# Differential attention: lambda's product moved to GpSimd, and VectorE's maxima and reciprocals put ahead of the difference and the lower halves

## The reference

```python
def diff_attention(q, k, v, lam):
    # q,k (B,H,2,S,d) holding (q1,q2)/(k1,k2); v (B,H,S,2d); causal
    ...
        logits = jnp.einsum('bhmqd,bhmkd->bhmqk', qi, k).astype(jnp.float32) * scale
        logits = jnp.where(kpos[None, :] <= qpos[:, None], logits, -jnp.inf)
        p = jax.nn.softmax(logits, axis=-1)
        pd = p[:, :, 0] - lam * p[:, :, 1]
        return jnp.einsum('bhqk,bhkd->bhqd', pd.astype(v.dtype), v)
```

## Time and profile before

| What | Value |
|---|---|
| median of 3 runs | 1244.85 us (1244.26 to 1247.47) |
| the profiled execution's own time | 1242.74 us |
| span of its trace | 1240.9 us |
| PE busy | 1202.0 us, 97% of the span |
| DVE busy | 748.2 us, 60% |
| ACT busy | 617.5 us, 50% |
| POOL busy | 139.8 us, 11% |
| differential stage | from about 218.3 us to 270.7 us of the span |

### The profile page before, as it was taken

One profiled execution on the slowest core, in us unless ns is written; L12 is line 12 of the kernel. 1 busy time (PEld: TensorE's weight loads), 2 busy tenths in 40 slices (PEclk: granted clock), 3 DMA queues, 4 the chain that ended last, 5 costly groups with the idle time before them and its releaser, 6 DMA issues.

```text
span 1240.9 us, 16231 instructions
## 1 busy us (share of the span) xinstructions
PE 1202.0 (97%) x6126; PEld 998.0 (80%) x6126; DVE 748.2 (60%) x1131; ACT 617.5 (50%) x1040; POOL 139.8 (11%) x217
## 2 busy tenths in 40 slices
PE   8999999989999999999999999999999999999997
PEld 6877788668888778888777888888898888888885
DVE  5556566764334364776276666445647848659478
ACT  5456686666233244643556544344347355354463
POOL 3023223110000011000033100010001000010011
PEclk9999999999999999999999999999999999999999
DMA  5422234113333535342113245312267474562732
GB/s 175 102 68 52 60 94 104 49 35 85 102 92 94 187 85 173 85 126 80 51 36 118 97 125 167 105 55 82 83 189 169 112 196 102 171 152 59 230 68 85
DMA packets 151740, 133.35 MB, mean 107 GB/s; under 512 B 5298, under 2 KB 124146, under 8 KB 151667
## 3 DMA queue, kind: packets, MB, share of 16 engines
q1 hardware_dynamic: 142528, 105.53, 28.9%
q0 software_dynamic: 3456, 12.58, 5.4%
q10 hardware_dynamic: 5682, 14.25, 3.3%
HBM read 115.55 MB, written 4.22 MB: 97 GB/s over the span
## 4 chain that ended last, share of the span: by engine, by line
PE 83%; DVE 8%; ACT 3%; DMA 3%; issue 1%; ACTq 0%; POOL 0%; POOLq 0%; DVEq 0%
PE lin L883 22%; PE lin L885 21%; PE lin L884 21%; DVE w_lo L2143 2%; PE tr L1041 2%; PE sc L885 2%; PE sc L884 2%; PE sc L883 2%; DVE neg_max L2168 1%; PE sc L1051 1%; PE tr L883 1%; PE tr L885 1%; PE tr L884 1%; PE sc L1053 1%; DMA x_m<-in_x 1%
## 5 line engine op out<-in xcount | busy, mean ns | idle before, releaser
L883 PE MATMUL lin<-h_hi,w_hi 128*128 128x512 f32 (+1 forms) x848 | 325.3, 384 | 5.0 <-DVE h_lo L2138 4.6
L885 PE MATMUL lin<-h_hi,w_lo 128*128 128x512 f32 (+1 forms) x848 | 317.4, 374 | 0.0
L884 PE MATMUL lin<-h_lo,w_hi 128*128 128x512 f32 (+1 forms) x848 | 317.0, 374 | 0.0
L2143 DVE TENSOR_TENSOR w_lo<-w_raw,w_hi 128x1024 fp32r<-128x1024 f32 x162 | 198.4, 1230 | 166.5 <-ACT w_hi L1452 154.9
L1452 ACT ACTIVATE w_hi<-w_raw 128x1024 fp32r<-128x1024 f32 x162 | 170.5, 1056 | 157.5 <-PE lin L885 53.7
L883 PEld LDWEIGHTS lin<-h_hi,w_hi 128*128 128x128 f32 x848 | 160.0, 189 | 33.7 <-DVE h_lo L2138 5.3
L885 PEld LDWEIGHTS lin<-h_hi,w_lo 128*128 128x128 f32 x848 | 159.8, 188 | 28.9
L884 PEld LDWEIGHTS lin<-h_lo,w_hi 128*128 128x128 f32 x848 | 160.2, 189 | 25.2 <-issue 0.2
L2168 DVE TENSOR_REDUCE neg_max<-sc 128x1 f32<-128x128 f32 (+3 forms) x112 | 52.2, 478 | 65.7 <-PE sc L1053 49.5
L1494 ACT ACTIVATE p<-sc,neg_max 128x128 f32<-128x128 f32 (+1 forms) x80 | 42.2, 528 | 72.6 <-DVE neg_max L2168 71.4
L883 PE MATMUL lin<-w_hi,h_hi 128*128 128x512 f32 x192 | 76.5, 398 | 1.2 <-DVE h_lo L2143 0.9
(11 more groups left out here) (354 smaller groups left out, 2310.0 us busy)
## 6 DMA issues: line engine op xcount, KB each, us to landing
w_raw<-in_w_in SPq DMA_DIRECT2D x74, 512.0 KB, 3.9
w_raw<-in_w_up SPq DMA_DIRECT2D x32, 512.0 KB, 4.4
wd_b<-in_w_down SPq DMA_DIRECT2D x24, 512.0 KB, 5.4
w_raw<-in_w_out SPq DMA_DIRECT2D x16, 512.0 KB, 3.5
w_raw<-in_w_xkv SPq DMA_DIRECT2D x16, 512.0 KB, 4.1
w_raw<-in_w_branch SPq DMA_DIRECT2D x8, 512.0 KB, 3.9
w_raw<-in_w_xq SPq DMA_DIRECT2D x8, 512.0 KB, 4.0
w_raw<-in_w_xo SPq DMA_DIRECT2D x8, 512.0 KB, 3.4
```

What stands on the lines that cost most here:

```text
L883: pe.matmul(o, lh, rh, start=start, stop=False)
L884: pe.matmul(o, lh, rl, start=False, stop=False)
L885: return pe.matmul(o, ll, rh, start=False, stop=stop)
L2143: return dve.tensor_tensor(out, x, as_f32(hi), ALU.subtract)
```

## The change

Five things are done. (1) On DVE the order inside a loop of the differential stage becomes maxima of w, reciprocals of w-1, difference of w-2, low part of w-5; before, the low part and the difference stood ahead of the maxima. (2) Lambda times the second reciprocal goes from DVE to POOL, 16 times, under a semaphore `lam_times`. (3) The first scores wait for their own head's queries and keys only, and the wait for the last tile of `vb` moves to the first value product; DVE takes that tile after the first maxima, and the weight split that followed it (of `zb`) moves some rounds into the stage on ACT and DVE; the same is done with the split after the second keys `ka` of fox. (4) ACT runs a one-column exponential after the forget gate and after the SiLU, and the table of exponentials is loaded there. (5) A group of `zb` filling is spread over 7 rounds and not 6.

```diff
-           "diff": [("zb", 0, 0, 6, 3)],
+           "diff": [("zb", 0, 0, 7, 3)],
...
             for w in range(16):
-                i, n = w % 4, P * (w % 4 + 1)
-                normalise(V0["diff"] + w, S0["diff"] + 2 * w, B["p0"][:, P_OFF[i]:P_OFF[i] + n])
+                i, n, s = w % 4, P * (w % 4 + 1), S0["diff"] + 2 * w
+                pool.wait_ge(s_rec, V0["diff"] + w + 1)
+                pool.tensor_scalar(rden[:, s + 1:s + 2], rden[:, s + 1:s + 2], neg_lam[:, :], 1.0, ALU.mult, ALU.mult)\
+                    .then_inc(lam_times, 1)
+                normalise(V0["diff"] + w, s, B["p0"][:, P_OFF[i]:P_OFF[i] + n])
...
-            pe.wait_ge(rope_lo, 8)
-            pe.wait_ge(k_twice, 16)
-            pe.wait_ge(dve_evac, DN[G["vb"][3]])
-
             def diff_scores(w):
                 h, i = w // 4, w % 4
+                if i == 0:
+                    pe.wait_ge(rope_lo, 5 + h)
+                    pe.wait_ge(k_twice, 8 + 2 * h + 2)
...
+                if h == 0:
+                    pe.wait_ge(dve_evac, DN[G["vb"][3]])
                 pe.wait_ge(tr_lo, R0["diff"] + 4 * h + 4)
...
+            def exponentials_next():
+
+                link(act.activation(act_one[:, :], ones[:, 0:1], ACT.Exp))
+
+            exponentials_next()
...
-            for c in range(2):
-                keys_hi("ka", c)
-                next_hi("ka", c)
+            keys_hi("ka", 0)
+            next_hi("ka", 0)
+            keys_hi("ka", 1)
...
+            def fox_exps(m):
+                causal_exps("fox", R0["fox"])(m)
+                if m == 4:
+                    next_hi("ka", 1)
...
             act.activation(B["y_1"][:, :, :], B["y_1"][:, :, :], ACT.Silu).then_inc(za_silu, 1)
+            exponentials_next()
...
-            next_hi("vb", 3)
...
+                if w == 2:
+                    next_hi("vb", 3)
...
+            def fox_max(m):
+                causal_max("fox")(m)
+                if m == 5:
+                    next_lo("ka", 1)
...
-            next_lo("vb", 3)
+
+            for t in range(NT - 1):
+                vb_lo(t)
...
                 dve.reciprocal(rden[:, s:s + 2], denom[:, s:s + 2]).then_inc(s_rec, 1)
-                dve.wait_ge(s_rec, V0["diff"] + w + 1)
-                link(dve.tensor_scalar(rden[:, s + 1:s + 2], rden[:, s + 1:s + 2], neg_lam[:, :], None, ALU.mult))
...
+                dve.wait_ge(lam_times, w + 1)
                 dve.wait_ge(s_norm, V0["diff"] + w + 1)
...
             for w in range(16 + 8):
+                if w < 16:
+                    diff_max(w)
+                if w == 0:
+                    vb_lo(NT - 1)
+                if 0 <= w - 1 < 16:
+                    diff_invert(w - 1)
+                if 0 <= w - 2 < 16:
+                    difference(w - 2)
+                if w == 3:
+                    next_lo("vb", 3)
                 if 0 <= w - 5 < 16:
                     probs_lo(R0["diff"] + w - 5, w - 5)
-                if 0 <= w - 2 < 16:
-                    difference(w - 2)
-                if w < 16:
-                    diff_max(w)
-                if 0 <= w - 1 < 16:
-                    diff_invert(w - 1)
```

More of the change, by code:

```diff
@@ L427, in two_blocks_kernel @@
         eps_n = sb("eps_n", [P, 2], F32)
+        act_one = sb("act_one", [P, 1], F32)
         sumsq = sb("sumsq", [P, 26, 2], F32)
@@ L473, in two_blocks_kernel @@
         lam_ready = sem("lam_ready")
+        lam_times = sem("lam_times")
         fa_ln = sem("fa_ln")
@@ L1657, in fox_split @@
                     next_hi("za", k - 4)
-            attention("fox", 32, lambda m: probs_hi(R0["fox"] + m, m, G["fox_pv"]), causal_exps("fox", R0["fox"]),
+            attention("fox", 32, lambda m: probs_hi(R0["fox"] + m, m, G["fox_pv"]), fox_exps,
                       stacked_out("fox_pv", fox_tmp), fox_fill, lambda end: 2,
@@ L2291, in _ @@
                 next_lo("qa", c)
-            for c in range(2):
-                keys_lo("ka", c)
-                next_lo("ka", c)
+            keys_lo("ka", 0)
+            next_lo("ka", 0)
+            keys_lo("ka", 1)
+            def fox_max(m):
+                causal_max("fox")(m)
+                if m == 5:
+                    next_lo("ka", 1)
             def fox_fill(k):
@@ L2304, in fox_split @@
                     next_lo("za", k - 4)
-            attention("fox", 32, causal_max("fox"), lambda m: probs_lo(R0["fox"] + m, m),
+            attention("fox", 32, fox_max, lambda m: probs_lo(R0["fox"] + m, m),
                       lambda m: invert(S0["fox"] + m), stacked_out("fox_pv", fox_tmp), fox_fill, lambda end: 3,
@@ L2337, in _, with vb_lo @@
                 next_lo("vb", q)
-            for t in range(NT):
+            def vb_lo(t):
                 after_scalar(G["vb"][t])
```

## The result

The changed kernel takes 1261.68 us (median of 4 runs, 1259.6 to 1264.88) against 1245.23 us: the ratio is 1.0132 with a 95% interval of 1.0102 to 1.0162. It is slower, and the time lies near the forecast (1260, range 1252 to 1273). The profiled execution took 1263.64 us, with a span of 1261.8 us.

The account below looks back on a forecast made before the run. PE bounds the kernel, busy 1202.0 of 1240.9 us. Terms -3.2 -1.0 +20.6 -0.7 (idle given back) -2.3 made +13.4 us, 1258.2 in terms of the median; +2 for clock gave 1260, range 1252 to 1273.

Parts of the forecast that it names:

- The chain on DVE: Rounds 5 to 15: PE's transposes wait for DVE's maximum, reciprocals, difference and low part; 1.87 us per round, +20.6 us.
- the second rival: Rounds 5 to 15: overlap or hidden hand-overs make waits 1.4 us, not 1.87; 1253 us without low clock; chance 0.11.
- The clock: Rounds 5 to 15: PE's busy share is at the edge of the lower clock level; two spells taken, +2 us.
- the first rival: Clock low for much of rounds 5 to 15: half of PE's work gives +13, 1271 us; chance 0.22 above 1264.
- its sign: Differential stage: a granted clock near 0.5 in many stretches would show low clock through much of the eleven rounds.
- my weighing of two rows: At the stage's entry, 1.64 us busy of 3.70 was followed by low clock; elsewhere 1.39 of 3.40 was not.
- The entry: Start of the differential stage: waits and the low clock after them go, less a late `w_lo`; -3.2 us.
- Fox's head: Start of fox: the 1.12 us wait for an exponential behind a weight split and table load goes; -1.0 us.
- The end: End of the differential stage: moved filling covers a 1.55 us wait, and the 1.64 us one shrinks to 0.9; -2.3 us.
- Lambda on POOL: Differential stage: 16 products at 0.3 us cost nothing, covered by at least 3 us before the difference; uncovered, 2 to 7 us.
- Sum: Whole kernel: all terms gave +13.4 us on the profiled execution's 1242.74; the clock added +2.
- rivals 2 to 4: Shorter chain, 1253 us, chance 0.11; no chain, 1237.7 us, chance 0.06; waits cancel, 1241.5 to 1248.5 us, chance 0.03.

Follow-up runs that it names:

- Low part first: Changed kernel with only DVE's low part put back ahead of the maxima, difference left late: 1242.24 us, ratio 0.9966 to the kernel before.
- filling first: Changed kernel with PE's filling unit ahead of the transposes in the differential stage: 1249.84 us, ratio 1.0028 to the kernel before.
- the exchange: Changed kernel with DVE's low part put ahead of the difference, both still behind the maxima: 1253.58 us, ratio 1.0052 to the kernel before.
- entry and tables alone: Kernel before with only the moved waits, value tile, weight splits and early table loads: 1243.59 us, ratio 0.9960.
- the old order: Changed kernel with DVE's low part and difference both back ahead of the maxima: 1243.65 us, ratio 0.9977 to the kernel before.
- low part and filling first: Changed kernel with DVE's low part ahead of the maxima and PE's filling unit ahead of the transposes: 1240.13 us, ratio 0.9950.
- the last one: Changed kernel with low part ahead of maxima, filling unit ahead of transposes, and `zb` filling back over 6 rounds: 1243.80 us, ratio 0.9968.

## Why the prediction was right, point by point

**The chain on DVE.** Right in mechanism, place and number of waits: they are in rounds 5 to 15, eleven, each for `pt_lo`, by the ring that the order rows showed. Low part first removes ten of them and halves the other, filling first and the exchange shorten them by what they should. The size was 1.87 us forecast per round and 1.59 measured (17.5 over eleven), 3.1 us too much in sum. DVE's rows in round 11 tell why: each member starts 0.07 to 0.08 us before the one ahead of it has ended (reciprocals 259.45, maxima until 259.53; difference 259.52, reciprocals until 259.60), so a sum of full durations counts each joint twice. That overlap is what the second rival names; the 1.59 lie between its 1.4 and my 1.87.

**The clock.** This is the term that was mis-sized. I took two spells of 1 us each and got four that cost 10.0 us, two of them of 10 and 7 us length. The step that failed is that a spell costs "about 1 where PE waits for nearly half of it", and the number of spells, two, was a guess. At the low level PE's own work takes nearly twice its time (in the spell of round 5 one filling matmul starts 0.42 us after the other, at 231.18 and 231.60; in round 10, at 1.00, it is 0.23 us, at 256.99 and 257.22), so PE is busy for most of a spell (9.02 of 11.00 us between 240 and 251), and value products with their 1.9 us fell into two of them and partly into a third. The 10.0 us are nearer to the first rival's +13 than to my +2, and its sign, a granted clock near 0.5 in several stretches, is there. So the first rival's mechanism was at work, and that the median, 1261.68, still came out 1.7 us from my 1260 is in part luck: the waits were 3.1 us too long in my sum and hid some of it.

The Trainium skill ("TensorE: Matmul & The Clock Gate", section "A second HAM failure mode: psum-queue depth-cycling") has frequent short idles between groups of matmuls make the clock swing between its levels. That was nearer to this trace than my weighing of two rows: waits of 1.40 to 1.80 us in each round did make it swing, and so did those of 0.87 to 1.40 in low part ahead of the difference. It is no rule for every such pattern, since the waits of 0.70 to 1.12 us in nine rounds of filling first left the clock at 1.00; and the drop behind the entry's one wait, which I counted as agreement, shows nothing of repeated idles.

Of the four executions of the changed kernel, those with a mean granted clock of 0.990 took 1259.6 and 1259.7 us, those with 0.988 and 0.985 took 1263.6 and 1264.9. The kernel before spreads in the same way: of its 81 executions beside the experiments, the seven with a clock of 0.996 took 1242.1 to 1243.5 us, the eleven with 0.989 took 1249.5 to 1251.6.

**The entry.** -3.2 us forecast; rounds 0 to 4 are 3.8 us shorter, of which 0.7 is a unit moved away: -3.1. **Fox's head.** -1.0 forecast, -1.3 measured. **The end.** -2.3 us forecast from waits; they fell from 3.2 to 0.55 us, -2.6, with a low spell of 1.6 us on top. The eleven rounds hid these gains in the changed kernel's time; entry and tables alone shows the first two by themselves (2.8 us of stage, and 1.3 from fox's first scores to the entry).

**Lambda on POOL.** Costed at nothing for PE, which is right in the changed kernel: the difference waits for POOL once, for 0.2 us. The price of one was taken as 0.3 us and is 0.52 (16 in 8.3 us), with one of 1.47 us outside the 0.2 to 0.6 that were named. The named price if the cover is gone, 2 to 7 us, showed up on DVE as 10 us of waits in the old order, and as 2.5 us of stage (51.2 against 48.7).

**Sum.** Forecast +13.4 without and +15.4 with the clock, against the profiled execution +20.9. What lies between +15.4 and +20.9 is waits -3.1, spells +8.0, a start 1.1 us later, and 0.5 less elsewhere. Two errors of opposite sign. Of the stage alone I said 13 to 16 us longer, and it is 21.5. The median, with executions of a higher granted clock in it, came to +16.5. The times of rivals 2 to 4 are out: no execution fell below 1259 us.

What stays open is why a spell starts when it does: the transposes of rounds 5 and 9 both wait for 1.53 us, but the first wait is followed by a spell and the second is not.

## What to carry to other kernels

Before an operation is moved back in an in-order queue, ask what on the other engines waits for it, and what the operations now ahead of it wait for; if the two are the same engine, the queues close to a ring that is paid in every round, however idle both engines are. Move only what the reason for the move asks for: here the later difference served the product on POOL, and the low part went along for nothing. Where such waits can't be avoided, put independent work of the waiting engine ahead of its wait, and count TensorE's clock as a price of its own: here it was 9.9 of the 21.5 us that the stage grew.

## What the runs showed of the hardware

The product of one column on POOL takes as long as DVE lets it. With nothing on DVE beside it, it takes 0.27 us (the first one of the changed kernel, at 220.93). In the changed kernel's round 11 it starts at 259.69 and ends at 260.11, 0.13 us after DVE's difference, which is busy from 259.52 to 259.98. Where DVE goes on with a weight split behind the difference, as in round 9 of the kernel with low part and filling first, it takes four times as long:

```profile
239.41 0.73 DVE L2387 SCALAR_TENSOR_TENSOR p<-px,rden,p 128x512 f32<-128x512 f32 x1
...
239.59 1.74 POOL L817 TENSOR_SCALAR rden<-rden,neg_lam 128x1 f32<-128x1 f32 x1 [2.52 <-DVE rden L2379]
...
240.06 1.22 DVE L2164 TENSOR_TENSOR w_lo<-w_raw,w_hi 128x1024 fp32r<-128x1024 f32 x1
```

It ends at 241.33, 0.05 us after the split (241.28). Both operations of DVE read two tensors from SBUF. The low part reads one of its two from PSUM (`tr`), and beside it the product takes its 0.27 us undisturbed, as at 236.55 in the rows of the old order above.

The Trainium skill ("GPSIMD Engine Reference", section "1. Specifications", the row on SBUF interfaces) says that POOL's are shared with VectorE, with contention when DVE's instruction has two SBUF inputs. The trace agrees, and shows that a tiny operation of POOL can be held for over a microsecond.

Filling idle time of TensorE with matmuls of no use made a kernel 10 us shorter in its stage, by the clock alone. And the low spells in other stages, which no edit here touches, differ from profile to profile (1.4 us of PE's time in the kernel before and 8.5 in the last one, between 300 and 760 us). No run shows why. That it is not the kernel alone is seen in the kernel before, whose executions spread from 1241.9 to 1251.6 us with the mean granted clock between 0.996 and 0.989. Differences of 0.3% between two kernels here have to be read with that in mind, and the length of a stage in the profile says more than the total.
